# POOL's split of each weight tile: a copy in place of a multiplication by ones, and its loops written out

## The reference

```python
proj = hn @ w_in                                   # block 1: 1024 -> 11280
merged = sigmoid(gate_dn) * (o_dn @ w_branch_dn) + sigmoid(gate_sb) * (o_sb @ w_branch_sb)
h = h + merged @ w_out
h = h + (silu(gate) * up) @ w_ffn_out              # gate, up = split(hn @ w_ffn_in)
...
mod = (c_act @ ada_w[i] + ada_b[i])                # block 2, for each of 2 layers: 1024 -> 6144, one row
qkv = h @ w_qkv;  o @ w_o                          # layer 0: attention
u = dwconv3(h @ w_in, conv_w, conv_b);  zc @ w_out # layer 1: long convolution by DFT
(silu(dwconv3(gate)) * val) @ w_down               # gate, val = split(h @ w_up), in both layers
```

## Time and profile before

| | us |
|---|---|
| median of 3 runs | 3760.74 (3753.86 to 3760.88) |
| profiled execution, from its first to its last instruction | 3739.3 |
| around that span, by the three runs | 14.6 to 21.6 |
| TensorE matmuls, busy | 3177.2 (85%) |
| DVE busy | 2209.4 (59%) |
| POOL busy | 2107.5 (56%) |
| ACT busy | 733.7 (20%) |

### The profile page before, as it was taken

How to read it: one execution, slowest core, us unless ns; L and a number is a source line. 1 busy time by engine, 2 the same in 40 slices (tenths; PEclk the granted TensorE clock), 3 DMA queues, 4 the chain that set the end, 5 groups by cost and what they waited for, 6 DMA issues and landing times.

```text
span 3739.3 us, 40173 instructions
## 1 busy us (share of the span) xinstructions
PE 3177.2 (85%) x14739; PEld 2448.1 (65%) x14739; DVE 2209.4 (59%) x2245; ACT 733.7 (20%) x1069; POOL 2107.5 (56%) x926
## 2 busy tenths in 40 slices
PE   7886898999779877778777998999989786699998
PEld 6775898789337755566665644677767544467776
DVE  5675654232332497777787554588338667538841
ACT  2253222432330001000000354111010111111100
POOL 5551322765018854566665502688867454368985
PEclk9897999999889987888888999999999898899999
DMA  3110000222002334444444100233222100023332
GB/s 101 56 57 29 1 0 0 79 75 72 0 0 89 120 113 129 117 116 127 132 135 121 57 0 12 79 90 90 93 66 78 59 28 15 23 68 90 90 100 69
DMA packets 365367, 259.46 MB, mean 69 GB/s; under 512 B 6330, under 2 KB 362263, under 8 KB 365005
## 3 DMA queue, kind: packets, MB, share of 16 engines
q1 hardware_dynamic: 361568, 248.53, 22.3%
q0 software_dynamic: 2256, 6.55, 0.6%
q10 hardware_dynamic: 1436, 2.96, 0.2%
HBM read 255.92 MB, written 2.10 MB: 69 GB/s over the span
## 4 chain that ended last, share of the span: by engine, by line
PE 59%; DVE 21%; DVEq 9%; issue 5%; ACT 3%; POOL 2%; POOLq 1%; DMA 1%; ACTq 0%
PE ps L487 13%; PE ps L488 13%; PE ps L489 13%; DVE adw L750 6%; DVEq L749 4%; DVE cv L1863 3%; PE ps L1364 2%; PE ps L1440 2%; PE ps L1344 2%; PE ps L1137 1%; PE ps L1150 1%; PE ps L578 1%; DVEq L2293 1%; PE ps L1247 1%; DVE SG L2247 1%
## 5 line engine op out<-in xcount | busy, mean ns | idle before, releaser
L659 POOL TENSOR_TENSOR spl<-raw,ones 128x1024 fp32r<-128x1024 f32 (+1 forms) x352 | 927.2, 2634 | 813.2 <-PE ps L489 732.3
L487 PE MATMUL ps<-HNH,spl 128*128 128x512 f32 (+1 forms) x2496 | 940.4, 377 | 121.2 <-DVE HNL L591 28.5
L661 POOL TENSOR_TENSOR spl<-raw,spl 128x1024 fp32r<-128x1024 f32 (+1 forms) x352 | 940.4, 2672 | 52.8 <-issue 3.8
L488 PE MATMUL ps<-HNL,spl 128*128 128x512 f32 (+1 forms) x2496 | 914.7, 366 | 0.0
L489 PE MATMUL ps<-HNH,spl 128*128 128x512 f32 (+1 forms) x2496 | 910.7, 365 | 0.0
L487 PEld LDWEIGHTS ps<-HNH,spl 128*128 128x128 f32 x2496 | 492.2, 197 | 243.2 <-issue 94.2
L488 PEld LDWEIGHTS ps<-HNL,spl 128*128 128x128 f32 x2496 | 493.1, 198 | 71.0 <-issue 4.3
L489 PEld LDWEIGHTS ps<-HNH,spl 128*128 128x128 f32 x2496 | 490.6, 197 | 74.0
L750 DVE TENSOR_TENSOR adw<-adw 128x512 f32<-128x512 f32 x192 | 266.8, 1390 | 14.3
L487 PE MATMUL ps<-AFH,spl 128*128 128x512 f32 x528 | 216.6, 410 | 5.3 <-issue 4.2
L2144 DVE SCALAR_TENSOR_TENSOR H<-ps,mod,H 128x512 f32<-128x512 f32 x32 | 24.0, 751 | 323.1 <-PE ps L489 323.1
(11 more groups left out here) (424 smaller groups left out, 5042.1 us busy)
## 6 DMA issues: line engine op xcount, KB each, us to landing
adw<-in_ada_w SPq DMA_DIRECT2D x96, 512.0 KB, 4.1
raw<-in_w_in SPq DMA_DIRECT2D x44, 1024.0 KB, 5.2
raw<-in_ffn_w_up SPq DMA_DIRECT2D x88, 512.0 KB, 4.7
raw<-in_w_ffn_in SPq DMA_DIRECT2D x44, 512.0 KB, 5.3
raw<-in_ffn_w_down SPq DMA_DIRECT2D x16, 1408.0 KB, 6.4
raw<-in_hy_w_in SPq DMA_DIRECT2D x12, 1024.0 KB, 5.1
raw<-in_w_ffn_out SPq DMA_DIRECT2D x8, 1408.0 KB, 7.7
raw<-in_w_branch_dn SPq DMA_DIRECT2D x8, 1024.0 KB, 5.1
```

Source lines behind the costliest of these rows:

```text
L487: pe.matmul(dst, w[0], x[0], start=first, stop=False)
L488: pe.matmul(dst, w[0], x[1], start=False, stop=False)
L659: pool.tensor_tensor(hi, w, heads_of(ones[:, :], gm.kt), ALU.mult)
L661: pool.tensor_tensor(lo, w, hi, ALU.subtract).then_inc(split_ready, 1)
```

## The change

In `pool_split` the rounded half is written by `tensor_copy`, which reads the weights alone, in place of a `tensor_tensor` multiplication that reads the weights and a tile of ones. The loop over the groups of slabs is written out for POOL alone: `i` is a plain number in every pass, and no hardware loop and no computed wait value is left in the split. The other engines keep their loops. The subtraction, the drain, the waits and their order stay. The two small products on `wab` (L845, L847) stay as they are.

```diff
         def pool_split(pool, gm):
 
-            for i, slabs in groups(pool, gm):
+            for i, slabs in [(n, range(min(R, gm.nslab - n * R))) for n in range(-(-gm.nslab // R))]:
                 seen = set()
                 for u, r, m in gm.units(len(slabs)):
...
                     pool.wait_ge(acc_ready, i * (2 * R) + (gm.u0 + u - 1))
                     w, hi, lo = gm.view(r)[:, :, m * P:(m + 1) * P], gm.half(u, 0), gm.half(u, 1)
-                    pool.tensor_tensor(hi, w, heads_of(ones[:, :], gm.kt), ALU.mult)
+                    pool.tensor_copy(hi, w)
                     pool.drain()
                     pool.tensor_tensor(lo, w, hi, ALU.subtract).then_inc(split_ready, 1)
```

## The result

| | before | after |
|---|---|---|
| median, 4 runs each, us | 3758.72 (3753.86 to 3760.88) | 3528.64 (3522.22 to 3534.93) |
| ratio, with 95% interval | | 0.9388 [0.9366, 0.9409] |
| profiled span, us | 3739.3 | 3526.7 |
| TensorE busy, us | 3177.2 | 3125.9 |
| mean granted clock | 0.916 | 0.935 |

The direction and the price of the copy came out as forecast. The size did not: the span lost 212.6 us where the terms added up to 112, and the median lies under the range's low end of 3590. (The medians differ by 230.1 us; the profiled execution of before was a short one, so its span understates the gain.)

A forecast was written before the change was run, and what follows sets the result against it. TensorE held 59% of the chain that ended last, DVE 30%, slowed by waits for POOL. Seven terms summed to 112 us off the 3739.3 span, giving 3627.3; with 21.4 around it, median 3649, range 3590 to 3742.

The forecast's parts named there:

- A: `ffn_in`, 11 pairs of slabs: multiplications in DVE's chain get shorter, 2.5 us a pair, 27 us.
- D: `dn_qk` and `dn_v`, 32 units: about half of the holds on DVE are by the multiplication, 22 us.
- G: `hy_in`: DVE's three-tap convolution beside 24 units gains 0.3 us each, 7 us.
- B: `ffn_out`, 4 pairs of outputs: three multiplications in each chain, 5 us a pair, 20 us.
- C: `gate_sb`, `branch_sb`, `mix_out`: about 14 multiplications in chains of modulation tiles and merges, somewhat over half counted, 12 us.
- F: `fc_in` of both layers: TensorE's lateness of 0.27 us a slab goes, 44 slabs, 12 us.
- E: Seven cold starts, such as `dn_z`, where TensorE waits for a first split or norm: somewhat over one saving each, 12 us.
- The first: Rival: the wait moves to the subtraction L661, DVE is held as long as before, about 3740 us; chance 0.10.
- Rivals 2: POOL's copy rounds slowly, at 1.5 to 1.9 us, half the saving, about 3705 us; chance 0.07.
- 3: Rival: POOL's copy costs what the multiplication did, only the loops change, 3760 us; chance 0.08.
- 4: Rival: POOL's copy is dearer than the multiplication and the kernel slower, up to 3960 us; chance 0.04.
- Rival 5: POOL's written-out program is fetched too slowly, stalls of 1.31 us, one in every four units deciding; chance 0.03 for slower.

The follow-up runs named there:

- e5: The changed kernel with the copy in `hy_in` only and the multiplication in all other stages, loops written out: 3710.48 us, 0.9894 of the kernel before.
- e2: The changed kernel with the multiplication kept in place of the copy, only POOL's loops written out: 3735.35 us, 0.9961 of the kernel before.
- e1: The changed kernel with hardware loops kept and an 8-element multiplication ahead of each copy: 3541.80 us, 0.9451 of the kernel before.
- e1w: The changed kernel, loops written out, with an 8-element multiplication added ahead of each copy: 3538.28 us, 0.9438 of the kernel before.
- e12: The changed kernel with the copy and the subtraction each issued in four pieces: 3473.50 us, 0.927 of the kernel before.
- e3: The changed kernel with a memset of `lo` (0.96 us, overwritten later) ahead of each copy: 3558.67 us, 0.9492 of the kernel before.

## Why the prediction was wrong

**The step that failed** is the one that priced terms A to D and G: it counted one saving of 1.48 us for each multiplication in DVE's chain, "of which as in A somewhat over half counts". In the traces a DVE instruction is not slowed in proportion to POOL's busy time. It is held once, for what is left of one POOL instruction, and how many are held depends on whether a POOL instruction is running when each comes. In the rows of `hy_in`, with 0.4 us of idle time a unit, every one was held; with 1.9, one of three is. There 1.4 us less POOL gave 4.2 us less DVE in the units that were fully held, 1.6 in the mean of all.

- **Second half of the same step: no threshold.** DVE's 8.4 us a unit in those rows lay above TensorE's 5.5 and fell below it. G, "0.3 each", rested on no row; it measured 28.5 / 24 = 1.19. The rows for it (three instructions of 2.6 us for each unit) stood in the trace of before, and I had not added them up. e5 shows that 27 of the 28.5 are the copy in that stage.
- **The clock and the busy products, put at nothing.** The prediction had the higher clock as room below and counted nothing. TensorE's busy time fell by 51 of the 212.6 us (7.9 us in `dn_qk`, where the granted clock went from 0.93 to 0.99), which is half as much as the 101 us that the terms lack. How much of it is the clock stays open, as said above.
- **A** (the stage is 376.8 us long, not the 371 of the window) was laid out again by hand and came to 2.5 a pair; it measured 4.0. My layout let the first L750 slip through and left the last L752 late; in the profile the whole first tile gets through. B measured 6.6 an output pair against 5; no two halvings of `ffn_out` take more than 5.06 after, and most take their 1.19 alone, where the earlier trace rows had 6.91.
- **C and D** were cut to about half by the same reasoning and measured about twice the term: 27.7 and 40.6. Of D's, 22.3 are in `dn_qk` and 15.9 between the first and the last split of `dn_v`; the recurrence behind moved by 2.4.
- **F** was read from one change of slab, 0.27 us. It measured 24.3 / 44 = 0.55, but 8.6 of the 24.3 are there in e2 already, which has the multiplication (264.0 and 264.1 us): of the 9.3 us that TensorE waited for DVE's L2253 in `fc_in[0]` before, none are left in e2. The copy's part is 15.7 / 44 = 0.36; the reading of 0.27 left out that the first product behind the pause is 0.1 longer (0.51). After, POOL's units start 5.5 apart and it stands idle about 1.9 ahead of each.
- **E** and everything else: 21.5 for 12. `dn_z`'s first wait fell from 7.23 to 5.64, the 1.5 of one saving.

**A second error, of 19 us, in the median.** I added 21.4 us for what lies around the span. Where runs list both, they differ by about 2: a run of the kernel before had 3746.05 beside a span of 3743.8. The 3739.3 of the profile was a short execution among runs that spread from 3733 to 3765 over the chips used here. So the miss of 120 us is 101 in the terms and 19 here.

**The rivals.** The first, the wait that moves to L661, is partly true: L665's mean rose from 966 to 1829 ns, L752's from 762 to 867, L2247's from 2455 to 2588. But L750's fell from 1390 to 931, and DVE's total by 333 us; it took back a part of the holds, not all. Rivals 2, 3 and 4 fell with the copy's 1079 ns. By the 1.8 cycles an element in the Trainium skill ("GPSIMD Engine Reference", section 3.1), which that page calls the best case, it would have been 1.54 us, an estimate; the trace has 1.04 and decides. Rival 5 fell with e1, e1w and e2. No rival had the case that came: a gain above the sum of the savings. I had 4.4 us "at most" for a pair of slabs and took such sums for upper ends, so the range ended at 3590.

**Right** were: where the gain would show (L750, TensorE's waits for L752, no lateness in `fc_in`), that L661 keeps its length (2454), that both attentions and the recurrence hardly move in length, and that no transfer matters.

**Open:** what sets which of DVE's instructions meets which of POOL's in `dn_qk` and the stages of C was not followed instruction by instruction; their lengths are measured, their cause is carried over from `ffn_in` and `hy_in`. How the 51 us of busy time divide between the clock and fewer pauses was not tried. Why the written-out loops give 0.4% with the multiplication and nothing with the copy was not tried further.

## What to carry to other kernels

Where two engines hold each other, add up DVE's held instructions for one unit of work and set the sum against the pace of the engine that should bound the stage; a saving on POOL can be worth up to one whole hold for every DVE instruction that then finds a gap, and most when the sum drops under that pace. Before asking for less work on the holding engine, ask for shorter single instructions: four pieces of the subtraction gave 84 us more here, as long as POOL's unit stays clearly below TensorE's (the subtraction grew from 2.45 to 3.7 us; at a unit of 5.5 us, in e12, 30 us were lost again). And take the distance between span and median from runs that list both.

## What the runs showed of the hardware

- POOL's copy that rounds to fp32r costs 1.04 us for 1024 elements when undisturbed, as the plain copy did; rounding is free in the one-input form as well.
- The hold goes both ways at the grain of one instruction: quarters of the subtraction take 0.74 us alone and 1.06 beside DVE's work (0.93 in the mean of all), while DVE's 0.75 us instructions take 0.97. Cutting it paid until POOL's unit came to 5.5 us.
- Cutting has a price of its own: four quarters take 4 x 0.74 = 2.96 us with nothing beside them, the whole 2.40.
- A POOL memset in the same place holds DVE's two-input instructions not at all; it holds the one-input forms (casts, tensor_scalar) as a copy does: in e3 the nine that began with over 0.4 us of it left ended 0.28 us behind it.
